# Token halves for the output projection, the first FF1 and the last FF2 of a decoder layer in float32 on one NeuronCore

## The reference, cut to what matters

```python
    mixed = jnp.sum(gate * proj, axis=2) @ w_out[l]           # 1024 x 1024
    x = x + rms_norm(mixed, norm_g[l, 1])
    h = rms_norm(x, norm_g[l, 2])
    f = jnp.square(jax.nn.relu(h @ w_ff1[l])) @ w_ff2[l]      # 1024 x 4096, 4096 x 1024
    x = x + rms_norm(f, norm_g[l, 3])
```

## Time and profile before

| | |
|---|---|
| device time, 3 runs | median 2168.74 us (2163.32 to 2169.66) |
| the profiled execution, its own device time | 2169.72 us |
| its span | 2167.8 us |
| PE / DVE / ACT / POOL busy | 93% / 42% / 34% / 5% of the span |

### The profile page before, as it was taken

How to read it: one execution, slowest core, us unless ns; L and a number is a source line. 1 busy time by engine, 2 the same in 40 slices (tenths; PEclk the granted TensorE clock), 3 DMA queues, 4 the chain that set the end, 5 groups by cost and what they waited for, 6 DMA issues and landing times.

```text
span 2167.8 us, 27272 instructions
## 1 busy us (share of the span) xinstructions
PE 2026.0 (93%) x10014; PEld 1611.8 (74%) x10014; DVE 903.5 (42%) x1202; ACT 736.1 (34%) x1125; POOL 101.6 (5%) x71
## 2 busy tenths in 40 slices
PE   7999999998999999998898999779999999999994
PEld 5886776677868778786586888558888888888883
DVE  5715456546244262541145562453223323323335
ACT  5325555444343343532233332333113103202310
POOL 0000000000203012030000000100000000000002
PEclk9999999999999999999899999889999999999997
DMA  4231221213031121212325433111111111111113
GB/s 162 101 107 69 87 76 70 87 67 127 20 121 44 39 107 39 77 39 104 135 97 195 136 122 142 59 58 48 50 47 48 48 48 48 48 48 49 48 39 155
DMA packets 52763, 174.18 MB, mean 80 GB/s; under 512 B 5744, under 2 KB 5744, under 8 KB 52720
## 3 DMA queue, kind: packets, MB, share of 16 engines
q1 hardware_dynamic: 51568, 171.52, 22.2%
q10 hardware_dynamic: 1152, 2.10, 0.3%
HBM read 127.45 MB, written 46.14 MB: 80 GB/s over the span
## 4 chain that ended last, share of the span: by engine, by line
PE 73%; DVE 6%; ACT 4%; issue 3%; DMA 3%; POOL 1%; SPq 1%; DVEq 0%; POOLq 0%; ACTq 0%
PE gemm L320 18%; PE gemm L322 18%; PE gemm L321 18%; PE dn L1187 2%; PE z L1083 2%; PE dn L1185 2%; PE gemm L1266 2%; DMA w_raw<-w_stream 2%; PE gemm L1267 2%; PE gemm L1268 2%; PE dn L1105 1%; DVE d_cv L1474 1%; ACT w_hi L307 1%; PE attn_out L1116 1%; PE cumsum L1116 1%
## 5 line engine op out<-in xcount | busy, mean ns | idle before, releaser
L320 PE MATMUL gemm<-act_hi,w_hi 128*128 128x512 f32 x1472 | 616.7, 419 | 18.4 <-DVE act_lo L501 10.2
L322 PE MATMUL gemm<-act_hi,w_lo 128*128 128x512 f32 x1472 | 580.4, 394 | 0.0
L321 PE MATMUL gemm<-act_lo,w_hi 128*128 128x512 f32 x1472 | 579.6, 394 | 0.0
L320 PEld LDWEIGHTS gemm<-act_hi,w_hi 128*128 128x128 f32 x1472 | 280.1, 190 | 94.5 <-issue 29.5
L312 DVE TENSOR_TENSOR w_lo<-w_raw,w_hi 128x1024 fp32r<-128x1024 f32 x142 | 175.1, 1233 | 398.0 <-ACT w_hi L307 393.1
L322 PEld LDWEIGHTS gemm<-act_hi,w_lo 128*128 128x128 f32 x1472 | 279.5, 190 | 61.1
L321 PEld LDWEIGHTS gemm<-act_lo,w_hi 128*128 128x128 f32 x1472 | 280.8, 191 | 54.2 <-issue 6.5
L307 ACT ACTIVATE w_hi<-w_raw 128x1024 fp32r<-128x1024 f32 x142 | 149.6, 1053 | 329.7 <-PE gemm L322 281.4
L320 PE MATMUL gemm<-f_hi,w_hi 128*128 128x512 f32 x512 | 199.2, 389 | 0.0
L321 PE MATMUL gemm<-f_lo,w_hi 128*128 128x512 f32 x512 | 199.2, 389 | 0.0
L322 PE MATMUL gemm<-f_hi,w_lo 128*128 128x512 f32 x512 | 199.2, 389 | 0.0
(11 more groups left out here) (231 smaller groups left out, 2374.7 us busy)
## 6 DMA issues: line engine op xcount, KB each, us to landing
w_raw<-w_stream SPq DMA_DIRECT2D x142, 512.0 KB, 3.6
projections<-stage SPq DMA_DIRECT2D x60, 512.0 KB, 2.9
gate<-projections SPq DMA_DIRECT2D x48, 256.0 KB, 2.7
d_in<-projections SPq DMA_DIRECT2D x12, 512.0 KB, 4.5
y_lo<-branch_outputs SPq DMA_DIRECT2D x6, 1024.0 KB, 11.9
x_sb<-xT SPq DMA_DIRECT2D x8, 512.0 KB, 9.6
x_fin<-xT SPq DMA_DIRECT2D x4, 1024.0 KB, 9.3
residual<-mixed SPq DMA_DIRECT2D x8, 512.0 KB, 2.6
```

The source lines that it names most:

```text
L320: nc.tensor.matmul(g_bank[hf][:], w_hi[s][:, k, :], a_hi[:, k, t], start=(k == 0), stop=False)
L321: nc.tensor.matmul(g_bank[hf][:], w_hi[s][:, k, :], a_lo[:, k, t], start=False, stop=False)
L322: last = nc.tensor.matmul(g_bank[hf][:], w_lo[s][:, k, :], a_hi[:, k, t], start=False, stop=(k == KT - 1))
```

## The change

The output projection, the first FF1 and the last FF2 run in half-blocks. All eight blocks are done for the tokens of half 0, then all eight again for half 1, and the weights are loaded and split for each pass. A half-block is 24 products and uses only the bank of its slot (`g_bank[s]`). The pairs of the stream become 48 turns (36 to 83), 12 of them loaded a second time.

- The barriers of phases 5, 6 and 7 are gone. SP waits for the end of the branch phase by semaphores and issues x as eight loads of 512 KB before it goes on with the weights.
- The chain behind the output projection (scale, add x, square, split for FF1) is done per tile and half by `x1_tiles` (DVE) and `take_x1` (ACT). Half 0's lies beside the projection's half 1, half 1's beside FF1's half 0. `TILES_AT` says which tiles go with which block.
- The second norm is no longer applied to `act_hi`, `act_lo`: they hold x times the gain, and its inverse root (`root_x1`) is multiplied in by DVE when it empties FF1's bank (`ff_root`). Relu moves to DVE and the square to ACT in all FF1 groups.
- x after the first residual is stored by DMAs that ACT issues, and read back into `act_hi` (`x_end`) at the start of the last FF2, ahead of later weights on SP.
- The last norm of half 0 (`scale_end`, `add_end`) lies beside half 1 of the last FF2. POOL has no part in it any more.

```diff
+        TILES_AT = [[], [0], [1, 2], [3], [4], [5], [6], [7]]
+        def half_product(pe, n, s, hf, a_hi, a_lo, fills, ready=None):
+            pe.wait_ge(lo_ready[s], n + 1)
+            pe.wait_ge(bank_read[s], 1 + fills)
+            t = half_of(hf)
+            for k in range(KT):
+                if ready is not None:
+                    pe.wait_ge(*ready(k))
+                nc.tensor.matmul(g_bank[s][:], w_hi[s][:, k, :], a_hi[:, k, t], start=(k == 0), stop=False)
...
+            last.then_inc(blk_done[s], 1)
...
+        def total_of(pe, hf, squares, added, total):
+            pe.wait_ge(*added)
+            nc.tensor.matmul(d_bank[hf][:], ones[:], squares[:, half_of(hf)], start=True, stop=True).then_inc(total, 1)
+        def inverse_norm(act, hf, out, total, ln, root):
+            act.wait_ge(total, hf + 1)
+            nc.scalar.activation(out[:, half_of(hf)], d_bank[hf][:], ACT.Ln, scale=1.0 / D, bias=eps).then_inc(ln, 1)
+            act.wait_ge(ln, hf + 1)
+            nc.scalar.activation(out[:, half_of(hf)], out[:, half_of(hf)], ACT.Exp, scale=-0.5).then_inc(root, 1)
...
 -            end_phase(sp, 5)
+            for s in range(2):
+                sp.wait_ge(blk_done[s], PAIR_OUT)
+            sp.wait_ge(ml_ready, 1 + KT)
+            for r in range(8):
...
+                sp.dma_start(x_fin[:, 2 * q:2 * q + 2, t], xT[2 * q:2 * q + 2, :, t].rearrange("k p s -> p k s")).then_inc(x_ld[r], 16)
...
+            stream(PAIR_OUT + 1, PAIR_OUT + 4, 0)
+            stream(PAIR_OUT + 4, PAIR_FF + 4, 4)
+            stream(PAIR_FF + 4, PAIR_LAST + 2, 8)
+            for s in range(2):
+                sp.wait_ge(blk_done[s], PAIR_LAST)
+            sp.wait_ge(x1_st, 16 * 2 * KT)
             for r in range(4):
...
+                sp.dma_start(x_end[:, 2 * r:2 * r + 2, :], x1T[2 * r:2 * r + 2].rearrange("k p s -> p k s")).then_inc(x1_back[r], 16)
+            stream(PAIR_LAST + 2, PAIR_LAST + 4, 8)
...
 +            def take_x1(hf, k):
...
+                act.wait_ge(x1_ready, c + 1)
...
+                nc.scalar.activation(c_sq[c % 2][:, 0:HALF], mixed[:, k, t], ACT.Square).then_inc(c_squared, 1)
+                nc.scalar.activation(act_hi[:, k, t], mixed[:, k, t], ACT.Copy, scale=cols[:, V_NORM + 16 + k:V_NORM + 17 + k]).then_inc(c_hi, 1)
+                act.dma_start(x1T[k, :, t], mixed[:, k, t]).then_inc(x1_st, 16)
+            for hf in range(2):
...
+                for b, n, s in half_pass(PAIR_OUT + 4 * hf):
...
+                    act.wait_ge(blk_done[s], n + 1)
+                    nc.scalar.activation(mixed[:, b, t], g_bank[s][:], ACT.Copy).then_inc(bank_read[s], 1)
+                    split_hi(act, n + 1, s)
...
+                    nc.scalar.activation(n_sq[s][:], mixed[:, b, t], ACT.Square).then_inc(o_sq, 1)
+                    if hf:
+                        if b == 0:
+                            inverse_norm(act, 0, root_out, o_total, o_ln, o_root)
+                        for k in TILES_AT[b]:
+                            take_x1(0, k)
...
 +                for b, n, s in half_pass(PAIR_FF + 4 * hf):
+                    half_product(pe, n, s, hf, act_hi, act_lo, FILLS_OUT + n - PAIR_OUT,
+                                 ready=(lambda k: (c_lo, KT * hf + k + 1)) if b == 0 else None)
+                    if b == 0:
+                        total_of(pe, hf, sum_x1, (c_added, 1 + 8 * hf + 8), c_total)
+                        if hf == 0:
+                            total_of(pe, 1, sum_sq, (o_added, 1 + 16), o_total)
...
 +            def x1_tiles(hf, b):
+                for k in TILES_AT[b]:
+                    scale_out(hf, k)
+                    if k:
+                        split_x1(hf, k - 1)
+                    add_x(hf, k)
+                if b == 7:
+                    split_x1(hf, KT - 1)
...
+            for hf in range(2):
+                for b, n, s in half_pass(PAIR_FF + 4 * hf):
+                    dve.wait_ge(blk_done[s], n + 1)
+                    if b == 0:
+                        dve.wait_ge(c_root, hf + 1)
+                    ff_root(hf, s, max(1, 1 + 8 * hf + b - 1))
+                    ff_lower(b, hf, s, 8 * hf + b)
+                    split_lo(dve, n + 1, s)
+                    if hf == 0:
+                        x1_tiles(1, b)
```

More of the change, by code:

```diff
@@ L590, in _ @@
                     load_weights(sp, 0, r, first=True)
[L591 removed]
+            for one in (*bank_read, *stored, dn_yst, *dn_taken, *y_stored, at_read, av_done, dn_chain, ml_ready, f_lr):
                 sp.sem_inc(one, 1)
@@ L714, in _, with stream @@
-            sp.wait_ge(out_st, 16 * KT)
+            for s in range(2):
+                sp.wait_ge(blk_done[s], PAIR_OUT)
+            sp.wait_ge(ml_ready, 1 + KT)
+            for r in range(8):
+                hf, q = divmod(r, 4)
+                t = half_of(hf)
+                sp.dma_start(x_fin[:, 2 * q:2 * q + 2, t], xT[2 * q:2 * q + 2, :, t].rearrange("k p s -> p k s")).then_inc(x_ld[r], 16)
+            def stream(first, end, back):
+                with sp.Fori(first, end) as n:
+                    for s in range(2):
+                        load_weights(sp, n, s, back=back)
@@ L717, in _ @@
+            stream(PAIR_LAST + 4, N_TURNS, 12)
+            for hf in range(2):
+                for k in range(KT):
+                    sp.wait_ge(out_ready, KT * hf + k + 1)
+                    sp.dma_start(outT[k, :, half_of(hf)], mixed[:, k, half_of(hf)]).then_inc(out_st, 16)
+            sp.wait_ge(out_st, 16 * 2 * KT)
         @block.scalar
@@ new lines, in _ @@
+            ff1(3)
+            for hf in range(2):
+                t = half_of(hf)
+                for b, n, s in half_pass(PAIR_LAST + 4 * hf):
+                    if n + 1 < N_TURNS:
+                        split_hi(act, n + 1, s)
+                    act.wait_ge(bank_read[s], 1 + FILLS_LAST + n - PAIR_LAST + 1)
+                    if 8 * hf + b >= 2:
+                        act.wait_ge(e_added, 1 + 8 * hf + b - 1)
+                    nc.scalar.activation(n_sq[s][:], mixed[:, b, t], ACT.Square).then_inc(e_sq, 1)
+                    if hf and b == 0:
+                        inverse_norm(act, 0, root_out, e_total, e_ln, e_root)
@@ L1279, in _ @@
-            leave_phase(pe)
-            def ff_group(g):
+            for hf in range(2):
+                for b, n, s in half_pass(PAIR_OUT + 4 * hf):
+                    first = (hf, b) == (0, 0)
+                    half_product(pe, n, s, hf, act_hi, act_lo, FILLS_OUT + n - PAIR_OUT,
+                                 ready=(lambda k: (ml_ready, 1 + k + 1)) if first else None)
+                    if hf and b == 0:
+                        total_of(pe, 0, sum_sq, (o_added, 1 + 8), o_total)
@@ L1291, in ff_group @@
[L1291 to L1298 removed]
+                        full_block(PAIR_FF2 - 4 + 8 * g + i, s, act_hi, act_lo)
+            ff2(0, lambda hf, k: (f_lr, 1 + 8 * hf + k + 1))
@@ new lines, in _ @@
+            with pe.Fori(1, 3) as g:
+                ff1(g)
+                ff2(g, lambda hf, k: (f_lr, 1 + 16 * g + 2 * k + hf + 1))
+            ff1(3)
+            for hf in range(2):
+                for b, n, s in half_pass(PAIR_LAST + 4 * hf):
+                    half_product(pe, n, s, hf, f_hi, f_lo, FILLS_LAST + n - PAIR_LAST,
+                                 ready=(lambda k: (f_lr, 1 + 48 + 2 * k + hf + 1)) if b == 0 else None)
+                    if hf and b == 0:
+                        total_of(pe, 0, sum_sq, (e_added, 1 + 8), e_total)
@@ L1692, in _ @@
+            dve.wait_ge(e_root, 2)
+            for k in range(KT + 1):
+                if k < KT:
+                    scale_end(1, k)
+                if k:
+                    add_end(1, k - 1)
         @block.gpsimd
```

387 lines of the change are left out of this document (166 added, 221 removed).

## The result

| | before | after |
|---|---|---|
| median, us | 2168.53 (4 runs, 2163.32 to 2169.66) | 2150.73 (4 runs, 2148.72 to 2153.5) |
| ratio | 1 | 0.9917, 95% interval 0.9898 to 0.9937 |
| profiled execution: span, device time | 2167.8, 2169.7 | 2149.9, 2151.8 |
| granted clock, mean of the span | 0.973 | 0.975 |

The account below looks back on a forecast made before the run. PE is the bound, busy 93%, with 90 us lost in the middle (55.5) and tail (34.5). Middle gives 1.7, tail 15.0: span 2133.0 + 19.5 = 2152.5, device time 2154.4, forecast 2154 us, range 2146 to 2164.

Parts of the forecast that it names:

- Step 1: Projection's half 0: PE resumes 11.6 us late, its weights behind the load of x, plus 2.5 of low clock: 14.1.
- The rival that the weights pass x: Projection's half 0: weights pass x or are split without a wait, 11.6 + 2.5 us fewer, 2140 us; chance 5%.
- Step 2: Projection's half 1: DVE and ACT loop of 6.9 us a block against 5.44; 5.9 us lost, low clock and ones included.
- Steps 2 and 4: Loops through DVE and ACT: 6.9 us a block in the projection's half 1, 7.7 in FF1's half 0, PE 5.44.
- Step 3: Into FF1: first half-block starts 1.4 us late and ends 8.9 late, waiting for tiles 6 and 7; `ff_root` at 1418.9.
- Step 6: FF2 to the last product: 609.4 us, plus 0.5 for weights behind x's read-back, plus 0.9 for ones, ending at 2133.0.
- Step 7: After the last product: only half 1 is left, POOL's additions gone; tail 19.5 us, a gain of 15.0.
- The rival with 1.2 GHz throughout: Blocks that carry tiles: the clock stays at 1.2 GHz, costing 35 us, 2189 us and slower; chance 4%.
- steps 3 to 5: Into FF1, FF1's half 0 (first to last bank 51.8 us) and half 1 (no tile); FF2 starts at 1522.2.
- a rival of 2%: Projection to FF2: both loops and the load stay hidden, the middle loses 20 us, 2120 us; chance 2%.

Follow-up runs that it names:

- e1: The changed kernel with SP issuing the weights of turn 37 ahead of the eight loads of x instead of behind them; 2131.9 us, ratio 0.9837.
- e8: The changed kernel with half 0's eight final tiles moved from beside the last products to behind the last sum of squares on DVE; 2155.1 us, ratio 0.9950.
- e4: The changed kernel with turn 37's weights ahead of x and each block's first residual tile ahead of DVE's operations that wait for ACT; 2105.4 us, ratio 0.9708.
- e9: e4 plus x1 read back piece by piece, x in pieces between weights, one tile per FF1 half 0 block, half 0's last tile earlier; 2100.5 us, ratio 0.9692.
- e3: The changed kernel with only DVE's order changed: a block's first residual tile goes ahead of the operations that wait for ACT; 2120.0 us, ratio 0.9771.

## Why the prediction was right, by its steps

| step | forecast | measured |
|---|---|---|
| 1, load of x | 11.6 + 2.5 = 14.1 | 12.8 + 2.8 = 15.6 |
| 2, half 1 of the projection | 5.9 (loop 6.9 a block) | 4.4 (loop 6.50) |
| 4, FF1's half 0: first to last bank | 51.8 (loop 7.7) | 50.4 (loop 7.20) |
| 3 to 5 together | 33.7 | 32.3 |
| to FF2 | 227.9 | 226.4 |
| 6, FF2 to the last product | 610.8 | 614.1 |
| 7, tail | 19.5 | 18.0 |

How the measured ones come about, from start to start: PE's sum of ones behind half 1's first block starts at 1355.90, so that block began at 1355.90 - 5.44 = 1350.46. Half 0 thus took 59.1 us, 15.6 above 43.5. Half 1's last block starts at 1392.91 and is done at 1398.35, so half 1 took 47.9, 4.4 above 43.5. From there to FF2 at 1517.73 it is 119.4 us, 32.3 above the 16 half-blocks of 87.0; the forecast had 1522.2 - 1401.5 - 87.0 = 33.7.

- **Step 1** held in place, cause and size. The rival that the weights pass x fell with the 14.61 us that ACT waited. PE resumed 12.8 us late, not 11.6. In the changed kernel the order is what holds the weights back, and e1 showed what the other order is worth: the rival's 14 us, and 2 more.
- **Step 2's total** came near by luck. Of its 5.9 us, 2.5 were a low stretch of the clock, and there was none in this half: all of its waits were short. The sum of ones took 0.45 us, not 0.87. The waits of PE, in turn, cost 3.9 us (1.8, 1.1 and 1.1), where the forecast had 2.2 and a few tenths.
- **Steps 2 and 4** held in kind: the loops are slower than PE's 5.44 us because the engines wait for each other. Each turn was forecast 0.4 to 0.5 us too long. The term that was mis-sized is the store issued by ACT, which I took as 0.24 us of ACT's time. In the rows above it stands beside the square (1444.23, ACTq) and costs none. The other 0.25 us is hand-overs: the square of `f_t` is followed after 0.65 us where I had 0.78, and `take_x1` begins 0.72 us behind the start of `add_x` where I had 0.84.
- **Step 3**: `ff_root` followed the projection's end after 17.0 us (1415.33 - 1398.35); the forecast had 17.4.
- **Step 6** was the largest miss, +3.3 us. The wait for the read-back was 1.84 us, which cost 2.1 from start to start, not 0.5 (+1.6), and a low clock came behind it: over the 5.3 us from 2063.7 the clock was 0.68, so 64% of them at half speed, 1.7 us. I had no low clock there, since I had a wait of 0.5 us. This one profile is an extreme: the stage took 614.2 us in it and 611.1 to 612.8 in the seven others with the same read-back, and 611.1 is where the forecast lay (610.8).
- **Step 7**: POOL gone and half 0's tiles beside PE, as forecast (e8). The tail was 1.5 us shorter: the ones took 1.14 us, not 1.4, the eight tiles 10.2 (2137.18 to 2147.39), not 10.8, the rest is hand-overs.
- **The clock**. The rival with 1.2 GHz throughout did not come. The clock was low behind each wait of 3.9 us or more and rose again within the same block or the next; six waits of 0.71 to 1.42 us left it full. The Trainium skill (TensorE: Matmul & The Clock Gate, HAM oscillation) describes a kernel that starts each step cold. The trace agrees for the long waits, at four places of the middle with 13.0 us in all, and not for the loops.
- **The sum.** Against the forecast: -2.9 at the start, where nothing was forecast (0.7 the barrier, the rest not the change's in any way that is known); +1.5 in step 1, -1.5 in step 2 and -1.4 in steps 3 to 5; +3.3 in step 6; -1.5 in the tail. It came out at 2151.8 for the profiled execution against 2154.4: -2.6. The errors largely cancelled, and that is luck; no single one would have left the range.

Where did the large gain go, then? The 54.8 us that PE lost behind 1382 vanished as intended (the forecast calls them a wait of 52), and 52.3 us are lost in the same stage after. The change set no limit to this: e4 and e9, with the same arithmetic and other orders, lose 9.8 and 6.5 us in it. Before the runs I had called the case in which the middle is largely freed a rival of 2%, at 2120, since it needed the engines to overlap "what the order makes them do in turn". For the change as it stood that was right; two edits of order are what it lacked.

Not settled: whether the low clock is what e1 and e3 share; what decides whether the clock falls behind a wait of 2 us (it did after 1.84, it did not after 1.85 in e3, after 2.09 in e4 and, in the kernel before, after 1.8); and why kernels of the old form reach the projection later.
